# Layer B of a hybrid decoder step: from a head at a time to groups of four chunks, with the recurrence of one group beside the matrices of the next

## What is computed

```python
conv = silu(sum_w xpad[:, w:w+T] * conv_w[w])      # xpad = 3 columns before + qkv = h @ w_in
q, k, v = split(conv); q = l2norm(q) * SCALE; k = l2norm(k)
beta = sigmoid(b); g = -exp(a_log) * softplus(a + dt_bias)
lmat = strict_lower((k*beta) @ k.T * decay)        # per chunk
u, w = solve(I + lmat, [v*beta, k*beta*exp(gc)])   # per chunk
aqk = (q @ k.T) * decay
step over chunks: v_new = u - w @ S
                  o = (q*exp(gc)) @ S + aqk @ v_new
                  S = S * exp(g_last) + kdec.T @ v_new
o = rmsnorm(o, o_norm_w)
```

## Time and profile before

| | us |
|---|---|
| median of three runs | 2793.62 |
| the profiled execution itself | 2792.09 |
| its span, first to last instruction | 2790.3 |
| units and convolution ahead of head 0 | 1348.9 to 1408.1 |
| heads 0 to 6 | 1408.1 to 2059.3 |
| head 7, matrices and inverse | 2059.3 to 2102.0 |
| head 7, recurrence | 2102.0 to 2132.5 |
| first unit of the next phase | 2141.3 |

### The profile page before, as it was taken

How to read it: one execution, slowest core, us unless ns; L and a number is a source line. 1 busy time by engine, 2 the same in 40 slices (tenths; PEclk the granted TensorE clock), 3 DMA queues, 4 the chain that set the end, 5 groups by cost and what they waited for, 6 DMA issues and landing times. The chain is left out here.

```text
span 2790.3 us, 45369 instructions
## 1 busy us (share of the span) xinstructions
PE 2509.1 (90%) x19392; PEld 1669.3 (60%) x19392; DVE 867.3 (31%) x2129; ACT 644.0 (23%) x1478; POOL 153.0 (5%) x194
## 2 busy tenths in 40 slices
PE   6899999999999884798998899889977999886998
PEld 4666666666666652344666666666655666682443
DVE  3012232232232330121254544555452122315011
ACT  3012312311311320111123322432231134300000
POOL 0100010010010020000111100110000000000000
PEclk8999999999999885798799999999997999756899
DMA  5631231311311155512530000000010110028210
GB/s 156 205 139 38 80 134 53 83 55 38 84 55 37 46 191 177 219 69 62 169 104 26 18 10 26 25 18 10 11 33 10 31 31 28 12 67 274 93 45 34
DMA packets 205005, 209.05 MB, mean 75 GB/s; under 512 B 13414, under 2 KB 172102, under 8 KB 204015
## 3 DMA queue, kind: packets, MB, share of 16 engines
q1 hardware_dynamic: 198518, 164.65, 19.1%
q0 software_dynamic: 6288, 41.51, 4.3%
HBM read 178.78 MB, written 67.18 MB: 88 GB/s over the span
## 5 line engine op out<-in xcount | busy, mean ns | idle before, releaser
L571 PE MATMUL bank<-arena 128*128 128x352 f32 x2304 | 715.0, 460 | 9.2 <-PEq L235 9.2
L571 PEld LDWEIGHTS bank<-arena 128*128 128x128 f32 x2304 | 425.2, 191 | 215.6 <-issue 12.0
L1433 PE MATMUL bank<-arena 128*128 128x352 f32 x1152 | 395.0, 470 | 2.7 <-PEq L235 2.7
L1108 PE MATMUL bank<-arena 128*128 128x512 f32 (+1 forms) x720 | 314.8, 598 | 3.9 <-PEq L235 3.9
L1433 PEld LDWEIGHTS bank<-arena 128*128 128x128 f32 x1152 | 199.8, 191 | 78.4 <-issue 4.8
L1108 PEld LDWEIGHTS bank<-arena 128*128 128x128 f32 (+1 forms) x720 | 130.5, 182 | 181.9 <-issue 181.7
L1865 PE MATMUL bank<-arena 128*128 128x352 f32 x768 | 233.5, 462 | 2.4 <-PEq L235 2.4
L1865 PEld LDWEIGHTS bank<-arena 128*128 128x128 f32 x768 | 145.4, 192 | 79.7 <-issue 4.4
L1453 PEld LDWEIGHTS bank<-arena 128*128 128x128 f32 x896 | 129.0, 205 | 78.8 <-ACT arena L1624 34.2
L1453 PE MATMUL bank<-arena 128*128 128x128 f32 x896 | 155.3, 302 | 21.1 <-ACT arena L1624 14.8
L1464 PEld LDWEIGHTS bank<-arena 128*32 128x32 f32 x8192 | 130.8, 108 | 60.2 <-issue 39.5
(11 more groups left out here) (310 smaller groups left out, 2497.5 us busy)
## 6 DMA issues: line engine op xcount, KB each, us to landing
arena<-in_w_in_a SPq DMA_DIRECT2D x48, 512.0 KB, 3.8
arena<-in_w_in_b SPq DMA_DIRECT2D x40, 512.0 KB, 3.9
arena<-in_cache_win_k SPq DMA_DIRECT2D x48, 256.0 KB, 4.6
arena<-in_cache_win_v SPq DMA_DIRECT2D x48, 256.0 KB, 8.1
out<-arena SPq DMA_DIRECT2D x40, 256.0 KB, 3.0
arena<-in_x_prompt SPq DMA_DIRECT2D x16, 512.0 KB, 4.2
arena<-in_w_mem_kv SPq DMA_DIRECT2D x16, 512.0 KB, 4.9
arena<-in_cache_mem_k SPq DMA_DIRECT2D x32, 256.0 KB, 7.4
```

Source lines behind the costliest of these rows:

```text
L571: m = nc.tensor.matmul(bank[part_][:, 0:PART], ring.slots[:, (B0 + b) % RING, k, :], part_in(k, part_), start=k == 0, stop=k == KD - 1)
L1108: i = nc.tensor.matmul(bank[half][0:rows(n), :], brT[:, k, n * P:n * P + rows(n)], wo[:, k, half * 512:(half + 1) * 512], start=k == 0, st ...
L1433: m = nc.tensor.matmul(bank[part_][:, 0:PART], ring.slots[:, (B1 + b) % RING, k, :], part_in(k, part_), start=k == 0, stop=k == KD - 1)
```

## The change

The loop over heads becomes a loop over 16 groups G (two per head) plus one more turn. A turn has 16 slots. In each slot TensorE does one step of the matrices or inverse of group G (four chunks), one or two units, one step of the recurrence of group G - 1, and one or two units. The order on ACT and DVE follows the same slots: DVE reads the inverse's step, then the recurrence's, then does one step of a convolution.

- A level of the inverse is done for one group of four chunks at a time: `x` in one slot, `zt` and `z` in the next.
- A turn has 36 units: three in each of slots 0 to 3, two in each of the others. `AHEAD` is 24 instead of 16, and in a head parts 0 and 1 of q, k, v come first, then the three parts 2. The three weight blocks of a head are thus all in use until late in the head.
- Convolution, silu, squares, sums, roots, logarithms and factors are done for four chunks (512 columns) and for group G + 2 or G + 1, inside the slots of group G: sums in slot 3, roots in 4, inverses in 5, logarithms in 6, factors in 7, outputs of group G - 2 in slot 9.
- The sample columns' convolution moves from DVE to POOL, seven multiplies and adds and some waits for each of q, k, v of a head. The two cache copies are issued after the first samples and squares.
- The first chunk of a head has no products with the zero state: `ks`, `qs` and the clearing of S are gone.
- LT and M are kept for four chunks only; the squares and the level buffers X lie in other places.

```diff
-    slots = {"prep": 5, "m": 3}
-    slots.update({f"l{k}{x}": 2 for k in range(1, LEVELS) for x in "ab"})
-    for c in range(NT):
-        for x, n in zip("abc", (2, 1, 1) if c < 6 else (3, 3, 2)):
-            slots[f"r{c}{x}"] = n
-    AHEAD = 16
+    RSLOT = {0: (0, "a"), 1: (0, "b"), 2: (0, "c"), 4: (1, "a"), 5: (1, "b"), 6: (1, "c"),
+             8: (2, "a"), 9: (2, "b"), 10: (2, "c"), 12: (3, "a"), 13: (3, "b"), 14: (3, "c")}
+    PREP = {0: ("rl", "ra"), 1: ("kt", "vt"), 2: ("kk", "qk"), 3: ("m",)}
+    AT_SS, AT_ROOTS, AT_INV, AT_LOGS, AT_FACTORS, AT_OT = 3, 4, 5, 6, 7, 9
+    PIECES = [(0, 0), (0, 1), (1, 0), (1, 1), (2, 0), (2, 1), (0, 2), (1, 2), (2, 2)]
+    AHEAD = 24
+    NORM_AT = 64
+    slots = [(1, 2)] * 4 + [(1, 1)] * 12
+    conv_at = [{1 + w + 4 * i + 3 * (i == 2): (i, w) for i in range(3) for w in range(CW)},
+               {w + 4 * i: (i, w) for i in range(3) for w in range(CW)}]
+    silu_at = [{7: 0, 9: 1, 15: 2}, {7: 0, 8: 1, 12: 2}]
...
+            # TensorE
+            for G in range(NG_ + 1):
+                for s in SLOTS:
+                    if G < NG_:
+                        matrix_step(G, s)
+                    if s == AT_SS and G + 1 < NG_:
+                        norms(G + 1)
+                    if s == AT_OT and G > 1:
+                        outputs(G - 2)
+                    for u in units_at(G, s, 0):
+                        unit(*u)
+                    if G and s in RSLOT:
+                        chunk_step(G - 1, s)
+                    for u in units_at(G, s, 1):
+                        unit(*u)
+            outputs(NG_ - 1)
...
+                elif x == "b":
+                    readout(pe, g, f"zt{LEVELS - 1}")
+                    if c:
+                        readout(pe, g, f"ks{c}")
+                    to(g, f"tr{c}", [(MT[:, c, :], r_sb[:, c % 2, :] if c else vb[:, c, :])])
+                elif x == "c":
+                    readout(pe, g, f"tr{c}")
+                    to(g, f"av{c}", [(AT[:, c, :], vn[:, c % 2, :])])
+                    to(g, f"su{c}", [(kdec[:, c, :], vn[:, c % 2, :])])
...
+            # VectorE
+            for G in range(NG_ + 1):
+                for s in SLOTS:
+                    if G < NG_:
+                        matrix_step(G, s)
+                    if s == AT_OT and G > 1:
+                        outputs(G - 2)
+                    if G and s in RSLOT:
+                        chunk_step(G - 1, s)
+                    if s == AT_INV:
+                        if G > 1:
+                            out_factors(G - 2)
+                        if G + 1 < NG_:
+                            norm_inverses(G + 1)
+                    if s == AT_FACTORS and G + 1 < NG_:
+                        factors(G + 1)
+                    if G + 2 < NG_ and s in conv_at[G % 2]:
+                        conv(G + 2, *conv_at[G % 2][s])
```

More of the change, by code:

```diff
@@ L1436, in unit, with bank_free @@
                     m.then_inc(pd if part_ < 2 else ring.used, 1)
[L1438 to L1444, removed]
+            def bank_free(g, name):
+                n = place[(g, name)]
                 if n >= NWB:
@@ L1454, in to, with to_tiles @@
                 m.then_inc(wk, 1)
[L1456 to L1464, removed]
+            def to_tiles(g, name, mms):
+                o = bank_free(g, name)
+                for c, (rows, l, r) in enumerate(mms):
+                    for i, p0 in enumerate(range(*rows, 32)):
+                        m = nc.tensor.matmul(o[p0:p0 + 32, c * P // 2:(c + 1) * P // 2], l[:, 32 * i:32 * i + 32], r,
@@ L1465, in to_tiles, with outputs @@
                                              start=True, stop=True)
                 m.then_inc(wk, 1)
[L1468 to L1484, removed]
+            def outputs(g):
+                pe.wait_ge(onm, g + 1)
+                to(g, "ot", [(o_sb[:, c, :], None) for c in range(*GR[g % 2])])
@@ L1547, in _ @@
-            tail(HB - 1)
+            for u in units[NORM_AT:PER_HEAD + AHEAD]:
+                unit(*u)
[3 more added lines that the diff above has]
+                        matrix_step(G, s)
+                    if s == AT_SS and G + 1 < NG_:
+                        norms(G + 1)
[6 more added lines that the diff above has]
+                    for u in units_at(G, s, 1):
+                        unit(*u)
@@ new lines, in _ @@
+            for G in range(NG_ + 1):
+                for s in SLOTS:
+                    if G < NG_:
+                        if s == 0:
+                            exps(G, "rl", LT, 0)
+                        elif s == 1:
+                            exps(G, "ra", AT, GR[G % 2][0])
+                        elif s == 3:
+                            b = left(act, G, "m")
+                            nc.scalar.copy(flat(M), b[:, :]).then_inc(rd_act, 1)
+                    if s == AT_ROOTS:
+                        if G > 1:
+                            out_roots(G - 2)
+                        if G + 1 < NG_:
+                            norm_roots(G + 1)
+                    if G and s in RSLOT:
+                        chunk_step(G - 1, s)
+                    for u in ended(units_at(G, s)):
+                        piece(*u)
+                    if s == AT_LOGS and G + 1 < NG_:
+                        norm_logs(G + 1)
+                    if G + 2 < NG_ and s in silu_at[G % 2]:
+                        silu(G + 2, silu_at[G % 2][s])
@@ L1637, in _ @@
+            out_roots(NG_ - 1)
         @block.vector
```

681 lines of the change are left out of this document (353 added, 328 removed).

## The result

The changed kernel takes 2728.31 us (median of four runs, 2726.09 to 2728.75), the kernel before 2793.88 us (four runs). The ratio is 0.976, 95% interval 0.9745 to 0.9779: 65.6 us faster. The forecast was 2745 us with a range of its own of 2735 to 2755; the result lies under that range, at the number of rival 1 (2727 us), and inside the range given for 8 in 10, 2718 to 2783. The profiled execution took 2728.75 us with a span of 2726.5 us, 63.8 us less than before. One run of the kernel before, 6335.61 us in the session of e5 to e7, was in the slow state and is left out of the ratios; all others named here were fast.

The account below looks back on a forecast made before the run. TensorE bounds the block, waiting mainly at head seams. Start 1408.8 plus turns and end (38.5, 531.1, 34.2, 29.6, 28.6, 13.6, 8.2) gives 2092.6 against 2141.3, 48.7 us less: 2745 us, range 2735 to 2755, 8 in 10 2718 to 2783.

Parts of the forecast that it names:

- rival 1: Whole block: hardly any new waits, turns 13 to 16 nearer to engine needs; 65 to 70 us less, 2727; 14%.
- the seam wait: Start of each full head: PE's 5.56 us wait for DVE's third factor goes, with 1.8 us of slow start.
- some 1.0 us of small waits: Per full head: small waits at MT and the bank changes, taken as gone, 1.0 us.
- 0.4 us per turn for new ones: Turns with units: small new waits add 0.4 us, making 44.3 us per turn.
- 1.7 for `vn`: Per head: PE's wait for ACT's copy `vn`, 1.7 us, taken as gone.
- The cost of a change of kind: 32-column blocks between units: 0.33 to 0.37 us each; 12 more blocks per head add 4.0 us.
- the caches' copies: First turn and a half: copies begin at about 1405 instead of 1358 and cost nothing.
- Rival 2: Clock falls to half in each turn and in turns 14 to 16: 47 us back, 2792, no change; 7%.
- Rival 3: Level slots: VectorE's in-order reads make PE wait; 0.4 us a slot is 62 us, 2807, slower; 8%.
- Rival 4: Slots 0 to 3 or slot 7: matrices or factors hold PE 1.5 to 2 us per turn, 2770; 21%.
- slot 7's factors: Tight slot 7: logarithm, factors, then convolution; x of slot 8 read 0.3 us before PE wants it.
- The 2759 us by that rule: Logarithm and factors: with the page's drain 1.4 us later, PE waits 1.1 us per turn, total 2759 us.

Follow-up runs that it names:

- e5: Kernel before with sums in chunk 6, logarithm and factors in chunk 7 ahead of the last silu, nothing interleaved: 0.9957 of the kernel before.
- e7: Changed kernel with both cache copies moved to the next phase, behind the sixth gating product: 2715.8 us, 0.9705 of the kernel before.
- e6: Changed kernel with one additional 512-column copy on VectorE in each level slot: 0.9764 of the kernel before.
- e3: Changed kernel with the x block of levels 1 to 5 cut in two by a unit: 0.984 of the kernel before.
- e1: Changed kernel with the cache copies issued first, right behind POOL's memsets: 0.9757 of the kernel before.
- e2: Changed kernel with the cache copies issued in turn 4: 0.9754 of the kernel before.
- e9: Changed kernel run again without any edit: 0.9758 of the kernel before.
- e8: Changed kernel with the next group's norms late (sums slot 11, roots 12, inverses 13, logarithms and factors 15): 0.9884 of the kernel before.
- e4: Changed kernel with the recurrence in 12 slots of its own behind the 16 of the next group, not interleaved: 1.0032 of the kernel before.

## Why the prediction held, and where its sum was off

The direction, the bound and the mechanism held: PE bounds the block, the seam wait and its slow clock went, the last recurrence of 30 us shrank to one of four chunks, doubled changes of matmul kind cost as counted. The result stands at rival 1's number, 14% by the prediction: the forecast put the chance on the wrong side of "new waits". Its own terms against the trace:

| step | forecast, us | measured, us | off |
|---|---|---|---|
| start of turn 0, from the span's start | 1408.8 | 1409.9 | +1.1 |
| turn 0 | 38.5 | 52.4 | +13.9 |
| turns 1 to 12 | 531.1 | 509.1 | -22.0 |
| turn 13 | 34.2 | 33.2 | -1.0 |
| turns 14, 15 | 58.2 | 52.7 | -5.5 |
| turn 16 and end | 21.8 | 16.4 | -5.4 |
| next phase's first unit | 2092.6 | 2073.7 | -18.9 |

That the sum came as near as 19 us is in part luck. Without turn 0 the terms were 33 us too high, and turn 0's +13.9 took 14 of them back. e7, where turn 0 takes 38.3 us as forecast, came to 2715.8 us, outside even the range for 8 in 10. Rival 1's 2727 us was met by the same chance: its 5 us for turns 1 to 12 came to 22.0, its 5 for turn 13 to 1.0, and its 10 for turns 14 and 15 to 5.5.

- **Turns 1 to 12.** The step "some 1.0 us of small waits" per head was mis-sized, and so was the 0.4 us per turn for new ones. Head by head, 94.2 - 84.93 = 9.3 us went. Take off 5.56 + 1.8 for the seam, 1.7 for `vn` and 0.4 for the first chunk, add 4.0 for the changes: 88.7. What is left, 3.8 us, is what was called 1.0. The trace of before shows 3.4 of it. By the starts of single matmuls, its blocks of zt and z took 2.22 us on average over five heads against 1.93 for the shortest (1.5 us per head), the blocks of four 128-column passes 0.51 against 0.445 (1.0), the sixteen of `kk`, `qk` 2.04 against 1.79 (0.5), and `m` waited 0.4. Waits inside blocks show in the lines of waits only in part. Ten of them, 4.0 us in these five heads or 0.8 per head, are listed as "issue": late instructions, which the earlier trace rows leaves out and the prediction did not count. New waits were none, even with VectorE loaded by 0.46 us more per slot (e6).
- **The cost of a change of kind** was right: 0.33 to 0.37 us forecast, 0.34 measured by itself (e3), for a block with its two changes. The rule in "TensorEngine Tiling (Array Packing)" of the Trainium skill, Key Properties, that changing the mode drains the engine, fits that number; the page itself gives no price. For 24 blocks it is 8 us of a head of 84.93.
- **Turn 0** failed at "at the cost of nothing go ... the caches' copies ... where one weight block is due". The block was looked at, TensorE's instructions were not. 686 matmuls and as many weight loads in a turn meet 50 us of full queues, and their instruction transfers come late. e1, e2 and e7 show that the 14 us belong to the copies' place, and e7 removes them.
- **Thin turns.** The clock stayed at full from turn 13 until 2068.5, where the sum took 3.7 us per chunk instead of 2.9, and the level was counted at 3.5 us where it takes 3.2. Rival 2 (the clock) is refuted for the turns with units and recurrence: no half-clock stretch in turns 1 to 13; the two of turn 0 came with the late instructions. The thin turns 14 and 15 had none in this profile and two of 3.4 us in the repeat (e9).
- **Rival 3** (in-order reading) is refuted by the empty list of waits, and e6 shows that there was room for 0.46 us more per slot. **Rival 4** (the seam inside the turn) did not come, but e8 shows it is near: it appears with the factors in slot 15. The forecast that slot 7's factors would fit was right: x of slot 8 is read at 1655.65 with no idle time ahead of it, and PE did not wait.
- ScalarE's drain of 1.38 us, from "ScalarE: Activation LUTs" of the Trainium skill, section "What ACT_TABLE_LOAD costs", does not show: the load at 1652.06 takes 1.28 us and the logarithm starts at 1653.36. The 2759 us by that rule did not come.

Where the gain came from: the parts don't add. The seam alone is worth 12 us in the old order (e5), early norms 34 us in the new one (e8), and without interleaving nothing is left (e4). Taking interleaving away costs (1.0032 - 0.9762) x 2793.9 = 75 us, all of the gain and 9 more: groups of four with early norms, but one after the other, are slower than the kernel before. Of these 75 us 9 are turn 0, where e4 lost more to late instructions. What the samples' move to POOL and the missing products of a head's first chunk are worth by themselves was not run. After the block, 649.0 us became 652.8 with the same instructions. But e1, e4, e6 and e8 took 648.5 to 649.1 there, and e2, e3 and e9 652.6 or 652.7, again with the same instructions, so these 3.8 us aren't tied to the change inside the block; what decides between the two is open.

## What to carry to other kernels

- When a busy engine waits at the seam of two iterations, look for the whole chain behind the wait before moving one link. Interleaving the serial part of one group with the parallel part of the next removed every wait in the turns with units; easing the first link alone gave a fifth.
- Before a large background transfer is moved, look at what the busy engine runs beside it, and at the queue of kind "instruction" in the list of DMA transfers: a stretch of short instructions and a ring with no block to spare each lost about 14 us, a stretch of long matmuls with its weights loaded lost nothing.
- A block of 32-column matmuls between full ones cost 0.34 us for its two changes. Blocks of both groups side by side would halve the 24 blocks per head, but also lengthen the runs of short instructions; this was not tried.

## What the runs showed of the hardware

- TensorE's idle stretches marked "issue" are late instructions: all 68 in the twelve profiles, from 1400 to 2150 us, end 0.9 to 1.6 us behind a 16 KB transfer of kind "instruction", and lie multiples of 256 matmuls and weight loads apart. Beside 8 copies of 2 MB (DMA share 0.99) they lasted up to 6.3 us; with nearly empty queues, in the kernel before, 0.2 to 1.9 us inside dense 32-column blocks. They did not come under long matmuls at 235 GB/s.
- The granted clock fell to half inside a gap of 6.29 us and behind one of 3.01, but not behind one of 0.89 (turn 0). With PE busy 43.06 of 52.70 us at short intervals in turns 14 and 15 it stayed at full in one profile and fell twice for 3.4 us in another.
- On 32 columns POOL's multiplies and adds took 366 to 475 ns on average, and with their copies the samples of a head cost some 11.5 us of POOL where 10 were estimated; no wait of PE in turns 1 to 12 leads to them.
